# A hybrid SSD / gMLP / MoE layer on one core: the token stage laid out channel-major

## The chip, the core and the metric

One core of a Trainium2 chip runs the whole layer in one launch, all in f32. The metric is device time in microseconds (us), the median of the runs shown; work on the host before and after the launch is not in it.

## The reference, cut to what matters

One layer over 4,096 prompt positions (32 tiles of 128 tokens) and 128 sample positions (8 streams of 16, tile 33). Per tile of tokens x (128 x 1024):

```python
h = rms_norm(x, norm1_g)
proj = h @ w_in                       # 1024 -> 2568 columns
z, xbc, dt_raw, gu, gv = split(proj, [512, 1536, 1544, 2056])
xbc = silu(causal_conv(xbc))          # depthwise, width 4, along tokens, 1024 channels: x 512, B 256, C 256
dt = softplus(dt_raw + dt_bias)       # 8 heads
y = ssd_scan(x, dt, -exp(a_log), B, C) + d_skip * x   # running sums of a*dt, decays, products, a state per head
ssd_out = group_rms(y * silu(z)) * ssm_norm_g
gmlp_out = gelu(gu) * (tril(w_spatial) @ layer_norm(gelu(gv)) + b_spatial)   # chunks of 128 tokens, 8 groups
x = x + concat(ssd_out, gmlp_out) @ w_out
x = x + hier_moe(rms_norm(x, norm2_g))   # top 1 of 4 groups, top 2 of its 8 experts (SwiGLU, 256 wide)
y = rms_norm(x, final_norm_g)
```

It also returns the last three rows that went into the convolution, the SSD states and the sample's v rows.

## The kernel before, in words

The program is written by hand per engine, with semaphores; each engine issues its list in order. It has a token stage (a turn per tile, 33 turns and a closing one) and an expert stage (blocks of 128 routed rows).

**Weights and constants.** `w_in` and `w_out` lie in one `arena` of SBUF, `w_in` as eight row chunks of 2,568 columns; SP loads it in five column groups and VectorE multiplies norm1's gain in (L973 to L977). GpSimd builds identity and masks (L1074 to L1103), small vectors come as rows and are turned by TensorE (L557), the spatial matrices are turned by TensorE and masked by VectorE (L567, L982).

**A turn of TensorE (`pe_turn`, L372)**, for tile i, with the projections of tile i+1 between:

1. eight transposes of `xbc` (token-major, 1,024 channels) to `TB`, which ScalarE copies to `xT`, channel-major, with a halo of three columns (L383, L594);
2. the running sums of a*dt over tokens and their totals (L388, L389), then two 512-column products with a matrix of ones that lay each head's running sum along a row, from `dec` = mask x a*dt that GpSimd wrote (L395, L1061);
3. the first half of the x/B/C projection of the next tile (`project`, L364: eight chunks, 512 columns, hT stationary, weights moving), eight transposes of h2 of the tile before, the second half of x/B/C;
4. B against C (L411), transposes of the activated x and B back to token-major (L416), the router (L490), the spatial mixing (L428), the SSD products (L436, L443, L447);
5. the gv projection, the ranks for routing (L498), the gu projection, eight transposes of x of tile i+2, scaled by its norm before (L457, L850), the z projection;
6. eight transposes of `ycat`, the dt projection of eight columns (L468), and the output projection (L478, two halves), which VectorE adds to `x_res` (L835).

A f32 product of 128 rows stands in the trace as two matmul records, each with a weight load; a transpose as one.

**VectorE (`dve_turn`, L734)** runs the convolution in four passes of eight operations (L758, L760) with h2 after the first, then the decays, the SSD elementwise work, routing (L884), gating, slots (L902), layer norm of v (L852) and the dt chain (L865). **ScalarE (`act_turn`, L577)** copies PSUM banks out and does the activations, among them Gelu of gv and gu (L643, L645), and the copies of the transposed `ycat` to `tT` (L654). **GpSimd (`pool_turn`)** does reciprocal roots, the softplus of dt and the slot scatters. **SP (`sp_turn`, L1117)** queues the loads of x (twice per tile: `x_in` for norm and projection, `x_res` for the residual) and the stores.

**The sample turn** (tile 33) first turns the cached rows, a second set of spatial matrices and 32 state blocks on TensorE (`pe_sample_setup`, L501), with copies by ScalarE.

**The expert stage** gathers 128 rows per block, multiplies with the expert's weights (three loads per expert), adds the residual and scatters each finished block twice, to the prompt's output and to the sample's, rows of the other kind being out of bounds (L1381).

Of the kernel before, what the change touches and what calls it, by code (L numbers as in the profile page):

```python
# [15 lines left out]
F32 = mybir.dt.float32  # L17
I32 = mybir.dt.int32
U32 = mybir.dt.uint32
# [17 lines left out]
CW = 4  # L37
INP = W + CD + H + 2 * W
# [11 lines left out]
N_ROWS = 6  # L50
N_CONST = 3 + 2 + 3 + 2 + 1

W_GROUPS = ((COL_X, 512), (COL_X + 512, 512 + H), (COL_GU, 512), (COL_GV, 512), (COL_Z, 512))
NINIT = NE * T // P // 8
NBLK = 2 * T // P + NE
EPS = 1e-6

# [41 lines left out]
LATER = 8192  # L99
# [6 lines left out]
def build(nc, x_prompt, x_sample, cache_conv, state_ssm, norm1_g, w_in, conv_w, conv_b, dt_bias, a_log,  # L106
          d_skip, ssm_norm_g, ln_v_g, ln_v_b, w_spatial, b_spatial, w_out, norm2_g,
          w_rg, b_rg, w_re, b_re, w_gate, w_up, w_down, final_norm_g,
          y_prompt, y_sample, conv_prompt, ssm_prompt, conv_sample, ssm_sample, gmlp_v_sample):
    ctx = ExitStack()  # L110
    with ctx:
# [6 lines left out]
        def sem(name):  # L118
            return ctx.enter_context(nc.semaphore(name))

# [12 lines left out]
        w_in_sb = arena[:, 0:W_IN].rearrange("p (k n) -> p k n", k=KD)  # L133
# [3 lines left out]
        ident = sb("ident", [P, P])  # L137
        tri = sb("tri", [P, P])
        stri = sb("stri", [P, P])
        tri_s = sb("tri_s", [P, P])  # L140
        blk_s = sb("blk_s", [P, P])
        ones = sb("ones", [P, P])
        row_s = sb("row_s", [P, SB])
        iota_g = sb("iota_g", [P, NG])
        iota_e = sb("iota_e", [P, NE])
        neg_half = sb("neg_half", [P, 2])
        tok_id = sb("tok_id", [P, 1])
        g2_b = sb("g2_b", [P, D])
        lng_b = sb("lng_b", [P, W])
        lnb_b = sb("lnb_b", [P, W])  # L150
        small_b = sb("small_b", [P, 3 * H])
        dtb_b, alog_b, dsk_b = (small_b[:, k * H:(k + 1) * H] for k in range(3))
        aneg_b = sb("aneg_b", [P, H])
        rb_b = sb("rb_b", [P, NR])
        wr_sb = sb("wr_sb", [P, KD, NR])
        wsT = sb("wsT", [P, H, P])
        slot_init = sb("slot_init", [P, NINIT, 2])
# [6 lines left out]
        xbc = sb("xbc", [P, CD])  # L164
        xT = sb("xT", [P, CB, P + CW - 1])
# [3 lines left out]
        gu = [sb("gu", [P, W])] * 2  # L169
        zz = [sb("zz", [P, W])] * 2  # L170
# [11 lines left out]
        rows = h2[0:NROW, 0:P]  # L182
        iota_i = ycat[:, 0:NR + 1].bitcast(I32)
        place_i = ycat[:, 64:64 + NINIT].bitcast(I32)
        slots32 = ycat[:, 0:NE].bitcast(I32)
        dt_t = sb("dt_t", [P, H])
        adt = sb("adt", [P, H])
# [24 lines left out]
        tok0 = sb("tok0", [P, 1])  # L212
        row_i = sb("row_i", [P, 1], I32)
        tok_i = sb("tok_i", [P, P], I32)
        wt = sb("wt", [P, P])
# [8 lines left out]
        dt_p, acs_p, tot_p = MB[:, 0:H], MB[:, H:2 * H], MB[:, 2 * H:3 * H]  # L224
# [3 lines left out]
        smp_bank = [SS[:, 0, :], SS[:, 1, :], YB[:, :]]  # L228

        names = """consts w_scaled eout_a cols_full cols_out ws_full ws_out
            xsq_ready xr_ready x_scaled xT_full xT_out
            proj0 proj1 proj_gv proj_gu proj_z xbc0_out xbc1_out gv_out gu_out z_out
            xbcT_full xbcT_out halo_saved conv_done zs_ready xc_ready cb_done xb_full xb_out
            dt_done dt_read lg_read cb_read rank_read dtneg_ready dtexp_ready dtrec_ready dt_ready trid_ready acs_done bcast_done
# [5 lines left out]
            smp_zero smp_cache_T smp_cache_out smp_ws_T smp_ws_out smp_st_T smp_st_out smp_masks smp_dec_full  # L242
            smp_dec_out smp_new stateT_full stateT_out
# [3 lines left out]
        x_loaded = [sem(f"x_loaded{u}") for u in range(2)]  # L247
        res_loaded = [sem(f"res_loaded{u}") for u in range(2)]
        win_loaded = [sem(f"win_loaded{k}") for k in range(len(W_GROUPS))]
        rows_loaded, const_loaded, wout_loaded = sem("rows_loaded"), sem("const_loaded"), sem("wout_loaded")  # L250
# [3 lines left out]
        smp_loaded = sem("smp_loaded")  # L254
        w_loaded, wd_loaded = sem("w_loaded"), sem("wd_loaded")
# [4 lines left out]
        gf_loaded, slots_set = (sem(n) for n in ("gf_loaded", "slots_set"))  # L260
        dve_step, pool_step = sem("dve_step"), sem("pool_step")

        x_tiles = x_prompt.rearrange("a (t p) d -> (a t) p d", p=P)
        y_tiles = y_prompt.rearrange("a (t p) d -> (a t) p d", p=P)
        x2_tiles = x2_d.rearrange("(t p) d -> t p d", p=P)
        h2_tiles = h2_d.rearrange("(t p) d -> t p d", p=P)
        first_tiles = first_d.rearrange("(t p) d -> t p d", p=P)
# [6 lines left out]
        def input_tile(t):  # L274
            if isinstance(t, int) and t == NP:
                return x_sample.rearrange("b l d -> (b l) d")
            return at_tile(x_tiles, t)


        used = [0]  # L280

        def flat_of(ap):
            return ap.rearrange("p a b -> p (a b)")
# [11 lines left out]
        wsT_s = take(H * P).rearrange("p (h t) -> p h t", h=H)  # L295
        ws_nat = take(H * P).rearrange("p (h t) -> p h t", h=H)
        xT_s = take(CB * SB * (SL + CW - 1)).rearrange("p (b q l) -> p b q l", b=CB, q=SB)
        cache_sb = take(CD)
        adt_e = take(W)
        st_dec = take(4 * SB)  # L300
        sample_end = used[0]
# [1351 lines left out]
```

## Time and profile before

| | us |
|---|---|
| runs | 3192.27, 3192.38, 3183.14 |
| median | 3192.27 |
| profiled execution, its own time | 3190.75 |
| its span in the profile | 3188.9 |

The span goes from the first to the last instruction of the profiled execution; the 1.9 us beside it are launch and end. Times in the trace count from the span's start. A steady turn and the chain through it are read from the view of the chain of waits; the table by stage gives busy time of each engine in a stretch and, as PEclk, the granted clock of TensorE as a share of 2.4 GHz.

### The profile page before, as it was taken

The page shows a single profiled execution, that of the slowest core. Times are in us where ns is not written, and L with a number is a line of the kernel's source. Part 1 is how long each engine was busy: PE and PEld are TensorE (multiplying, and loading weights), DVE is VectorE, ACT ScalarE, POOL GpSimd, SP SyncE. Part 2 cuts the span into 40 slices and gives each one's busy share as a digit, 9 for nine tenths or more (in the row PEclk, how much of TensorE's full clock was granted, in tenths as well). Part 3 has the DMA queues.
Part 4 walks back from the last instruction along what each step waited for, and adds up shares of the span by engine and source line. Part 5 has one row for each costly group of instructions (what it writes and reads, how often), then busy time and mean ns, then how long its engine had stood idle before and what let it go on. Part 6 is the DMA issues. An engine that isn't in the chain of part 4 may idle for free.

```text
span 3188.9 us, 37210 instructions
## 1 busy us (share of the span) xinstructions
PE 3107.2 (97%) x10721; PEld 1686.5 (53%) x10721; DVE 1624.8 (51%) x4412; ACT 876.7 (27%) x1599; POOL 1087.5 (34%) x1988
## 2 busy tenths in 40 slices
PE   7999999999999999999999999996899999999997
PEld 3555565555555555555555555554444444444443
DVE  4454555456554555455544654456344444444444
ACT  2222332223232322233222322221122222222222
POOL 1112112221122112211221111110377767777776
PEclk9999999999999999999999999997899999999999
DMA  7011101101011111010110111023877666767754
GB/s 260 34 40 34 60 33 33 40 33 59 33 40 33 60 33 40 33 60 33 36 37 33 59 34 33 27 72 105 282 236 254 206 207 224 237 198 256 267 170 127
DMA packets 190380, 326.15 MB, mean 102 GB/s; under 512 B 52988, under 2 KB 125241, under 8 KB 190220
## 3 DMA queue, kind: packets, MB, share of 16 engines
q1 hardware_dynamic: 118220, 210.81, 19.5%
q0 software_dynamic: 72000, 113.62, 11.0%
q8 instruction: 50, 0.82, 0.1%
q14 instruction: 110, 0.90, 0.1%
HBM read 283.13 MB, written 182.14 MB: 146 GB/s over the span
## 4 chain that ended last, share of the span: by engine, by line
PE 95%; DVE 1%; DMA 1%; issue 1%; SPq 0%; ACT 0%; POOL 0%; POOLq 0%; DVEq 0%; ACTq 0%
PE PB L369 35%; PE PB L1448 18%; PE PB L478 14%; PE SS L1487 9%; PE TB L358 3%; PE TB L1436 2%; PE YB L436 2%; PE MB L490 2%; PE PB L428 2%; PE SS L395 2%; PE MB L369 2%; PE SS L443 1%; PE SS L447 1%; PE TB L416 1%; PE YB L1480 1%
## 5 line engine op out<-in xcount | busy, mean ns | idle before, releaser
L369 PE MATMUL PB<-arena,hT 128*128 128x512 f32 x2640 | 1164.9, 594 | 3.4 <-DVE arena L976 3.4
L369 PEld LDWEIGHTS PB<-arena,hT 128*128 128x128 f32 x2640 | 495.7, 191 | 578.5 <-issue 574.1
L1448 PE MATMUL PB<-arena,hT 128*128 x1296 | 571.6, 594 | 0.7 <-DMA arena<-in_w_down 0.7
L1001 POOL TENSOR_TENSOR spare<-neg_half 128x1 f32<-128x1 f32 x520 | 102.2, 197 | 1068.4 <-ACT hT L668 615.5
L478 PE MATMUL PB<-arena,tT 128*128 128x512 f32 x1056 | 461.5, 595 | 0.7 <-ACT tT L654 0.7
L1448 PEld LDWEIGHTS PB<-arena,hT 128*128 128x128 f32 x1296 | 247.0, 191 | 312.0 <-issue 312.0
L478 PEld LDWEIGHTS PB<-arena,tT 128*128 128x128 f32 x1056 | 198.1, 190 | 237.7 <-issue 236.8
L1487 PE MATMUL SS<-arena,xdt 128*128 x640 | 287.9, 592 | 0.0
L835 DVE TENSOR_TENSOR x_res<-x_res,PB 128x512 f32<-128x512 f32 x66 | 45.3, 687 | 397.0 <-PE PB L478 397.0
L760 DVE SCALAR_TENSOR_TENSOR xc<-xT,cols,xc 128x128 f32<-128x128 f32 x768 | 210.0, 346 | 2.3
L1362 POOL DMA_INDIRECT out<-arena,lng_b x160 | 171.7, 1073 | 49.2 <-issue 44.9
L1487 PEld LDWEIGHTS SS<-arena,xdt 128*128 128x128 f32 x640 | 115.4, 190 | 114.8 <-issue 114.8
L1516 ACT ACTIVATE xdt<-YB 128x256 f32<-128x256 f32 x80 | 30.7, 384 | 512.1 <-PE YB L1480 512.1
L594 ACT ACTIVATE xT<-TB 128x512 f32<-128x512 f32 x64 | 34.9, 595 | 429.5 <-PE TB L358 429.5
L1545 DVE TENSOR_TENSOR gv<-ycat,PB 128x256 f32<-128x256 f32 x81 | 34.1, 421 | 223.5 <-ACT ycat L1511 222.9
L1048 POOL TENSOR_TENSOR dtw<-dtw 128x8 f32<-128x8 f32 x33 | 6.7, 202 | 346.6 <-DVE dtw L874 346.6
L1005 POOL TENSOR_SCALAR rs<-sq 128x1 f32<-128x1 f32 (+1 forms) x99 | 19.4, 195 | 308.6 <-ACT hT L668 126.3
L1553 DVE SCALAR_TENSOR_TENSOR arena<-arena,rs 128x1024 f32<-128x1024 f32 x80 | 102.4, 1279 | 26.0 <-POOL rs L1389 25.4
L868 DVE TENSOR_TENSOR dtw<-MB,small_b 128x8 f32<-128x8 f32 x33 | 5.5, 167 | 205.1 <-PE MB L369 205.1
L758 DVE TENSOR_SCALAR xc<-xT,cols 128x128 f32<-128x128 f32 x256 | 69.4, 344 | 45.5 <-issue 28.9
L1071 POOL DMA_INDIRECT slot_tokens<-slots x66 | 71.4, 1082 | 48.9 <-DVE tok_id L930 34.5
L775 DVE TENSOR_SCALAR dec<-SS,e_in 128x128 f32<-128x128 f32 x264 | 86.9, 400 | 0.0
(320 smaller groups left out, 4220.2 us busy)
## 6 DMA issues: line engine op xcount, KB each, us to landing
arena<-in_w_gate SPq DMA_DIRECT2D x32, 1024.0 KB
arena<-in_w_up SPq DMA_DIRECT2D x32, 1024.0 KB
arena<-in_w_down SPq DMA_DIRECT2D x32, 1024.0 KB
h_rows<-h SPq DMA_DIRECT2D x34, 512.0 KB, 3.6
x_rows<-x_res SPq DMA_DIRECT2D x33, 512.0 KB, 2.6
first_rows<-g_b SPq DMA_DIRECT2D x33, 512.0 KB, 4.6
x_in<-in_x_prompt SPq DMA_DIRECT2D x32, 512.0 KB, 4.0
x_res<-in_x_prompt SPq DMA_DIRECT2D x32, 512.0 KB, 4.4
```

What stands on the lines that cost most here:

```text
L358: mm = nc.tensor.transpose(TB[b][:, k, :], src(4 * b + k), ident[:])
L369: mm = nc.tensor.matmul(out, hT[u][:, k, :], w_in_sb[:, k, col:col + n], start=k == 0, stop=k == KD - 1)
L478: mm = nc.tensor.matmul(PB[b][:, :], tT[:, k, :], w_out_sb[:, k, b * 512:(b + 1) * 512], start=k == 0, stop=k == KD - 1)
L758: ins = V.tensor_scalar(dst, src, tap[:, w, c:c + 1], cols[:, R_CBIAS + c:R_CBIAS + c + 1], ALU.mult, ALU.add)
L760: ins = V.scalar_tensor_tensor(out=dst, in0=src, scalar=tap[:, w, c:c + 1], in1=dst, op0=ALU.mult, op1=ALU.add)
L775: ins = V.tensor_scalar(dec[:, h, :], SS[:, h // 4, (h % 4) * P:(h % 4 + 1) * P], a, a, ALU.min, ALU.subtract)
L1001: nc.gpsimd.tensor_tensor(spare[:, k:k + 1], neg_half[:, 0:1], neg_half[:, 0:1], ALU.mult)
L1071: nc.gpsimd.indirect_dma_start(out=slot_d[:, :], out_offset=bass.IndirectOffsetOnAxis(ap=slots[:, k:k + 1], axis=0), in_=slots_f[:, 2 + 2 ...
L1362: nc.gpsimd.indirect_dma_start(out=dram, in_=src, in_offset=None, bounds_check=last, oob_is_err=False, out_offset=bass.IndirectOffsetOnAxi ...
L1448: mm = nc.tensor.matmul(PB[u][:, :], hT[u][:, k, :], arena[:, bass.ds(slot + k * 2 * DE, 2 * DE)], start=k == 0, stop=k == KD - 1)
L1487: mm = nc.tensor.matmul(SS[:, n, :], hTb[:, k, :], arena[:, bass.ds(slot + KD * 2 * DE + k * D + n * 512, 512)], start=k == 0, stop=k == 1)
L1553: V.scalar_tensor_tensor(out=f_buf[u], in0=f_buf[u], scalar=rs[:, u:u + 1], in1=gf_b, op0=ALU.mult, op1=ALU.mult).then_inc(s["fin_out"], 1)
```

## The change

- **Host layout.** All inputs come laid out: `x` as rows and once more turned (`x_cols`, per tile the channels in partitions), weights per group with each partition's data in one run, masks, identity and vectors as finished tables, spatial matrices and sample states already turned, gate, up and down of an expert in one array. Outputs y, states and conv rows come back in the kernel's layout and are rearranged on the host; y is one tensor, so a block is scattered once.
- **Turned x.** SP loads `x_cols` straight to hT, once z of the tile before has been projected. TensorE spreads the token's norm factor along a row by one transpose of a repeated column (`pe_spread`), VectorE multiplies hT by it. The eight transposes of x and ScalarE's two copies go.
- **x/B/C channel-major.** `project_channels` takes the weights as stationary operand, 128 channels at a time, and hT as the moving one, 128 columns. ScalarE copies the result straight to `xT`, of which there are two; the eight transposes of `xbc` go.
- **dt.** The gv projection is split: 256 columns of gv together with the eight of dt, and the other 256. The separate dt projection between the transposes of `ycat` and the output projection goes.
- **Running sums.** The sums go to `e_in` after the convolution's first pass; eight transposes of repeated columns spread them, and the totals are read from the last column. GpSimd's product for `dec`, the two products with ones and the product for totals go (the totals stay in the sample turn).
- **Order.** h2 moves behind the convolution's second pass; the spatial mixing writes to `TB[0]`; the first gv half stands between router and mixing; x of tile i+2 is scaled behind the last part of `ycat`.

The new and changed parts of the turn:

```diff
+        def project_channels(pe, u, b, name, done, waits):
+            for sm, v in waits:
+                pe.wait_ge(s[sm], v)
+            for c in range(4):
+                for k in range(KD):
+                    mm = nc.tensor.matmul(PB[b][:, c * P:(c + 1) * P], w_group(name)[:, k, c * P:(c + 1) * P], hT[u][:, k, :],
+                                          start=k == 0, stop=k == KD - 1)
+            mm.then_inc(s[done], 1)
+
+        def pe_spread(pe, t, waits):
+            pe.wait_ge(s["xr_ready"], t + 1)
+            for sm, v in waits:
+                pe.wait_ge(s[sm], v)
+            nc.tensor.transpose(TB[1][:, 0, :], rs[:, 0:1].broadcast_to([P, P]), ident).then_inc(s["rbc_full"], 1)
...
-            transpose8(pe, block_of(xbc), lambda b: [(f"xbc{b}_out", i + 1)] + before(b), "xbcT_full")
-            nc.tensor.matmul(acs_p, cum[:], adt[:], start=True, stop=True)
-            nc.tensor.matmul(tot_p, tot[:], adt[:], start=True, stop=True).then_inc(s["acs_done"], 1)
-            for b in range(2):
-                mm = nc.tensor.matmul(SS[:, b, :], tot[:], flat(dec[:, half(b), :]), start=True, stop=True)
-            mm.then_inc(s["bcast_done"], 1)
+            mm = nc.tensor.matmul(acs_p, tri_s if tn.sample else tri, adt[:], start=True, stop=True)
...
+                project_channels(pe, v, 0, "xa", "proj_xa",
+                                 [("x_scaled", i + 2), ("gu_out", 1) if tn.first else ("x2_half", 2 * i - 1)])
+            pe.wait_ge(s["acs_out"], i + 1)
+            for h in range(H):
+                mm = nc.tensor.transpose(bcast_p[:, h, :], e_in[:, h:h + 1].broadcast_to([P, P]), ident)
+            mm.then_inc(s["bcast_done"], 1)
...
+                project_channels(pe, v, 1, "xb", "proj_xb", [("z_out", 1) if tn.first else ("x2_half", 2 * i)])
...
+            if tn.next:
+                project(pe, v, PB[0][:, 0:NVA], "va", "proj_va", [("xa_out", i + 2)])
...
             if tn.next:
-                project(pe, v, PB[1][:, :], COL_GV, 512, "proj_gv", [("xbc1_out", i + 2)])
+                project(pe, v, PB[1][:, 0:256], "vb", "proj_vb", [("xb_evicted", i + 2)])
...
-                project(pe, v, PB[0][:, :], COL_GU, 512, "proj_gu", [("ycat_hi", i + 1)])
+                project(pe, v, PB[0][:, :], "u", "proj_u", [("va_out", i + 2)])
             if tn.next2:
-                pe.wait_ge(s["x_scaled"], i + 3)
-                transpose8(pe, block_of(x_in[u]), lambda b: [("xb_out", 2 * i + 1 + b)], "xT_full")
+                pe_spread(pe, i + 2, [("xb_out", 2 * i + 2)])
...
-            if tn.next:
-                project(pe, v, dt_p, COL_DT, H, "dt_done", [("cb_read", 1) if tn.first else ("rank_read", i)])
             pe.wait_ge(s["ycT_out"], 2 * (i + 1))
...
+        def act_va(act, t):
+            act.wait_ge(s["proj_va"], t + 1)
+            nc.scalar.activation(gv[:, 0:256], PB[0][:, 0:256], ACT.Gelu_apprx_tanh)
+            nc.scalar.activation(dt_raw[:, :], PB[0][:, 256:NVA], ACT.Copy).then_inc(s["va_out"], 1)
...
+            if tn.next:
+                act.wait_ge(s["mixed_done"], i + 1)
+                act.wait_ge(s["dt_read"], i + 1)
+                act_va(act, i + 1)
+                act_vb(act, i + 1)
...
+                if w == CW - 1:
+                    dve.wait_ge(s["acs_done"], i + 1)
+                    V.tensor_copy(e_in[:, 0:2 * H] if tn.sample else e_in[:, 0:H],
+                                  MB[:, H:3 * H] if tn.sample else acs_p).then_inc(s["acs_out"], 1)
+                if w == CW - 2 and tn.prev:
                     dve_h2(dve, i - 1, v)
...
-            V.tensor_scalar(x_in[u][:, :], x_in[u][:, :], rs[:, 0:1], None, ALU.mult).then_inc(s["x_scaled"], 1)
+        def dve_scale_x(dve, t, j, u):
+            dve.wait_ge(s["rbc_full"], t + 1)
+            dve.wait_ge(xt_loaded[u], 16 * (j + 1))
+            V.tensor_tensor(hT[u][:, :, :], hT[u][:, :, :], TB[1][:, 0:1, :].broadcast_to([P, KD, P]), ALU.mult).then_inc(s["x_scaled"], 1)
...
-            g.tensor_tensor(dec[:, :, :], over(mask, H), adt[:, :].rearrange("p (h a) -> p h a", a=1).broadcast_to([P, H, P]),
-                            ALU.mult).then_inc(s["trid_ready"], 1)
...
+            if tn.next2:
+                sp.wait_ge(s["proj_z"], i + 1)
+                sp.dma_start(flat(hT[u][:, :, :]), at_tile(x_cols, i + 2)).then_inc(xt_loaded[u], 16)
             if tn.next3:
-                sp.wait_ge(s["xT_full"], 2 * (i + 2))
-                sp.dma_start(x_in[v][:, :], input_tile(i + 3)).then_inc(x_loaded[v], 16)
+                sp.wait_ge(s["xsq_ready"], i + 2)
+                sp.dma_start(x_in[v][:, :], at_tile(x_rows, i + 3)).then_inc(x_loaded[v], 16)
...
+                sp.dma_start(xT_s[:, :, :, 0:HALO], cache_in.rearrange("p (b q w) -> p b q w", b=CB, q=SB)).then_inc(cache_loaded, 16)
...
+                sp.dma_start(conv_sample.rearrange("p (b q w) -> p b q w", b=CB, q=SB), xT_s[:, :, :, SL:]).then_inc(convs_stored, 16)
```

## Rows read from the trace of the kernel before

**Rows 1.** The page, part 1: busy us, share of the span, instructions.
```profile
PE 3107.2 (97%) x10721; PEld 1686.5 (53%) x10721; DVE 1624.8 (51%) x4412; ACT 876.7 (27%) x1599; POOL 1087.5 (34%) x1988
```

**Rows 2.** Busy time by stage: stretch, its length, PE, PEld, DVE, ACT, POOL, PEclk, DMA share.
```profile
62.38:128.00 65.62, 64.74 (x211) 35.37 (x212) 28.63 (x74) 16.93 (x28) 7.33 (x20) 0.95 0.03 8
128.00:192.40 64.40, 64.40 (x241) 36.10 (x240) 34.73 (x114) 19.25 (x33) 10.11 (x24) 1.00 0.12 42
2135.10:2204.75 69.65, 56.02 (x227) 39.05 (x227) 41.20 (x121) 17.80 (x44) 5.93 (x7) 0.80 0.08 28
2249.83:3165.00 915.17, 915.17 (x2716) 449.47 (x2717) 425.53 (x488) 226.04 (x474) 640.15 (x625) 1.00 0.68 225
```

**Rows 3.** The chain of waits in one steady turn: start us, us, what.
```profile
971.30 0.87 PE TB L358 x8
...
972.30 0.22 PE MB L389 x2
972.52 1.82 PE SS L395 x4
974.34 6.87 PE PB L369 x16
...
988.95 0.45 PE MB L411 x4
...
991.95 1.81 PE PB L428 x16
...
995.54 0.92 PE SS L443 x4
...
1011.51 0.88 PE TB L358 x8
...
1020.12 1.69 PE MB L369 x16
...
1035.64 0.87 PE TB L358 x8
```

**Rows 4.** The timeline of ScalarE in the turn after it: start us, us, what.
```profile
1063.19 0.19 ACT L668 ACTIVATION_READ_ACCUMULATOR hT<-x_in 128x1 f32 x1
...
1070.60 1.28 ACT L643 ACT_TABLE_LOAD   x1
...
1084.12 1.08 ACT L654 ACTIVATE tT<-TB 128x512 f32<-128x512 f32 x2
```

**Rows 5.** The timeline of VectorE at the turn of two tiles.
```profile
1035.68 0.69 DVE L835 TENSOR_TENSOR x_res<-x_res,PB 128x512 f32<-128x512 f32 x1 [6.11 <-PE PB L478]
1037.24 2.17 DVE L758 TENSOR_SCALAR xc<-xT,cols 128x128 f32<-128x128 f32 x8 [0.87 <-ACT xT L594]
```

**Rows 6.** The chain, the output projections before and after the long turn.
```profile
760.99 13.84 PE PB L478 x32
...
828.63 13.85 PE PB L478 x32
```

**Rows 7.** Busy time in one stretch of that turn, columns as in rows 2.
```profile
797.00:801.00 4.00, 4.00 (x20) 4.00 (x20) 3.44 (x18) 0.00 (x0) 0.00 (x0) 0.50 0.00 0
```

**Rows 8.** The timeline of TensorE at the start.
```profile
16.90 9.66 PE L369 MATMUL PB<-arena,hT 128*128 128x512 f32 x16 [1.83 <-DVE arena L976]
28.15 20.87 PE L369 MATMUL PB<-arena,hT 128*128 128x512 f32 x48 [1.59 <-DVE arena L976]
...
62.38 1.42 PE L358 MATMUL TB<-ident,xbc 128*128 128x128 f32 x8 [3.84 <-DVE wsT L984]
```

**Rows 9.** The timeline of VectorE at the start, scaling the last weights.
```profile
40.88 3.26 DVE L976 TENSOR_SCALAR arena<-arena,cols 128x512 f32<-128x512 f32 x8 [2.12 <-DMA arena<-in_w_in]
```

**Rows 10.** The chain at the start of the sample turn.
```profile
2135.24 0.60 PE SS L506 x8
...
2144.86 2.17 DVE xc L758 x8
```

**Rows 11.** The timeline of GpSimd in the tail.
```profile
3183.61 0.98 POOL L1362 DMA_INDIRECT out<-arena,lng_b  x1 [0.31 <-issue]
```

More of the change, by code:

```diff
@@ L163, in build @@
         hT = [sb(f"hT{u}", [P, KD, P]) for u in range(2)]
-        xbc = sb("xbc", [P, CD])
-        xT = sb("xT", [P, CB, P + CW - 1])
+        xT_mem = [sb(f"xT{u}", [P, CB * SB * (SL + HALO)]) for u in range(2)]
+        xT = [m[:, 0:CB * (P + HALO)].rearrange("p (b t) -> p b t", b=CB) for m in xT_mem]
+        xT_s = xT_mem[0][:, :].rearrange("p (b q l) -> p b q l", b=CB, q=SB)
         xc = sb("xc", [P, CB, P])
@@ L362, in block_of, with project @@
             return lambda c: t[:, c * P:(c + 1) * P]
-        def project(pe, u, out, col, n, done, waits):
+        def project(pe, u, out, name, done, waits):
             for sm, v in waits:
@@ L732, in heads, with over @@
             return ap.rearrange("p (h d) -> p h d", h=H)
+        def over(mask, n):
+            return mask.rearrange("p (a t) -> p a t", a=1).broadcast_to([P, n, P])
         def dve_turn(dve, st, tn):
@@ L983, in dve_phase1 @@
-            for b in range(2):
-                V.tensor_tensor(wsT[:, half(b), :], SS[:, b, :].rearrange("p (h t) -> p h t", h=4), over(tri, 4),
-                                ALU.mult).then_inc(s["ws_out"], 1)
+            dve.wait_ge(ws_loaded, 16)
+            V.tensor_tensor(wsT[:, :, :], wsT[:, :, :], over(tri, H), ALU.mult).then_inc(s["ws_ready"], 1)
             dve.wait_ge(wout_loaded, 16)
@@ L1650, with whole, layer, by_chunk @@
-    build(nc, *args)
-    r = _run(nc, [arrays], core_ids=[0])
-    return tuple(r.results[0][f"out_{i}"] for i in range(len(_OUTS)))
+    def whole(name):
+        return np.asarray(inputs[name])
+    def layer(name):
+        return whole(name)[0]
+    def by_chunk(w):
+        return w.reshape(-1, P, w.shape[-1]).transpose(1, 0, 2)
+    def spread(rows):
+        return np.broadcast_to(rows.reshape(1, -1), (P, rows.size))
+    x = np.concatenate([whole("x_prompt").reshape(SEQ, D), whole("x_sample").reshape(P, D)]).reshape(NT, P, D)
@@ new lines @@
+    w_in = by_chunk(layer("w_in"))
+    b_spatial, ws = layer("b_spatial"), layer("w_spatial")
+    ws_smp = np.zeros((H, P, P), np.float32)
+    for q in range(SB):
+        ws_smp[:, q * SL:(q + 1) * SL, q * SL:(q + 1) * SL] = ws[:, 0:SL, 0:SL]
+    state = layer("state_ssm")
+    lane = np.arange(P)
+    consts = np.zeros((P, NCONST), np.float32)
+    stream = lane // SL
+    same = stream[:, None] == stream[None, :]
+    upper = lane[:, None] <= lane[None, :]
+    for c, mask in ((C_IDENT, lane[:, None] == lane[None, :]), (C_TRI, upper), (C_STRI, lane[:, None] < lane[None, :]),
+                    (C_TRI_S, upper & same), (C_BLK_S, same), (C_ONES, same | ~same)):
+        consts[:, c:c + P] = mask
```

715 lines of the change are left out of this document (310 added, 405 removed).

## The prediction

> **What bounds the kernel now.** I read the page first. TensorE is busy for 97% of the span [rows 1], so the next question is whether it is held up anywhere or simply has that much to issue. The table by stage answers it [rows 2]: in a token turn TensorE is busy for all 64.40 us, while VectorE needs 34.73, ScalarE 19.25 and GpSimd 10.11 and the DMA engines work 12% of the time; in the expert stage it is busy for all 915.17 us. The places where it is not are the sample turn (56.02 of 69.65), the start and the tail. The chain of waits then gives a price for each piece [rows 3]: in a steady turn the chain never leaves TensorE, each piece starts where the one before ended, and from one first piece to the next are 1035.64 - 971.30 = 64.34 us. So a turn costs the sum of what TensorE issues, in its written order, and an edit is worth what it takes out of that sum, as long as no other engine becomes late.
>
> **A turn, term by term** (prices from [rows 3]). Taken out: the eight transposes of xbc (0.87) and of x_in (0.88), the dt projection of eight columns (1.69, as dear as a wide one per weight load), the second running-sum product (0.22) and the two ones-products that spread the sums (1.82). Together 5.48. Put in: eight transposes for the spread, 0.87 by the xbc row, and one of 1/8 of that, 0.11, for the scale row. The gv projection becomes halves of 264 and 256 columns: a pass of 512 takes 6.87/16 = 0.429, half of it 0.215; the 256-column row gives 0.92/4 = 0.23. I take 0.215 and 0.222, since sixteen in a row run like the long one: 7.0 instead of 6.87, +0.12.
>
> The x/B/C projections are the term that the trace does not show at length. Each goes from 16 passes of 512 columns (6.87) to 64 passes of 128, each with a weight load of its own. Bounds: from below 6.87, the same columns with the loads wholly hidden; from above, first the nearest row, the 128-column products of one turn, four passes in 0.45, 0.1125 each, 64 x 0.1125 = 7.20. The transposes run 128 columns at 0.87/8 = 0.109. I take 0.11, so 7.04 each, +0.34 for both. That loads hide behind streaming is seen in the same row: passes of 8 columns cost 1.69/16 = 0.106 and of 64 columns 1.81/16 = 0.113, about what a load alone needs, and 128 columns cost no more, though they stream for a quarter of 0.429 = 0.107 by themselves.
>
> The Trainium skill ("TensorE: Matmul & The Clock Gate", Part 3, The mechanism) says otherwise: weight loads overlap running matmuls only when they address another row group, which full-array matmuls never do. By that rule the change would lose its gain several times over; it is the first rival below. The trace does not agree: 0.1125 for load and streaming together [rows 3].
>
> One wait is new. Today the dt projection stands between the transposes of ycat and the output projection, and covers ScalarE's copies of them to tT. Those copies, 1.08 us from 1084.12, end at 1085.20 [rows 4]; the transposes end at the start of the dt piece, one turn after 1020.12 [rows 3], at 1084.47. With dt gone TensorE stands idle for some 0.8 us there (nothing, if the copies came earlier; 0.8 follows from the rows, so I take it). The sum is -5.48 + 0.98 + 0.12 + 0.34 + 0.80 = -3.24, a turn of 61.1 us.
>
> **Is another engine late in the new order?** Counting TensorE's pieces from the start of a turn: sums 0.1, x 7.2, spread 8.0, h2 8.9, B/C 15.9, the small products and router to 18.9, v-with-dt 22.5, mixing 24.3, the SSD products 27.9, second v half 31.3, ranks, u from 31.7 to 38.6, z to 45.6. VectorE starts the convolution straight after the last residual add (0.73 later, [rows 5]) instead of waiting for transposes and copies (1.6), four passes of 2.17 [rows 5]; h2 now stands after the second pass and is ready at about 6.7 (0.73, two passes, the sums and h2's own 1.3), needed at 8.0. The sums leave PSUM after the first pass, at 3.2, needed at 7.2. The convolution ends at 11 and the activated xc at 12, needed at 15.9. The tightest is u, which overwrites the bank of the first v half: ScalarE must have mixing behind it (24.3) and the square of x_in, which today ends at 1063.38 [rows 4], 27.7 into the turn, and not later in the new one; then it loads its table (1.28, [rows 4]) and evicts v and dt (some 0.8): 29.8, needed at 31.7. GpSimd loses its large product for dec; its dt chain keeps its place beside the output projection. The new wait on SP, for z before the load of the turned x, holds back only loads that are wanted a turn later; the extra 512 KB per turn meet DMA engines at 12% [rows 2]. Scaling hT (two 512-column VectorE operations' worth, about 1.3) waits for the spread at 38.7 and is done by 40, before the last transposes need its bank at 46. So these edits cost nothing beyond the sum; what covers them is TensorE's own queue, and the first to break would be u, with 1.9 us to spare.
>
> **The clock.** Four of the turns are about 3.3 us longer: from 760.99 to 828.63 are 67.64 [rows 6], with a granted clock of 0.50 (the 1.2 GHz level) [rows 7] just after router and mixing, the two pieces with the fewest columns, stood next to each other. All four make 12.6 (2007.1 from 128.0 [rows 2] to 2135.1 less 31 x 64.34). In the new order the v half with its 264 columns stands between them, so I count all 12.6 as gone; the bound is that they stay.
>
> **Outside the loop.** Start: TensorE begins its first projection at 16.90 and the first turn at 62.38 [rows 8]. What goes: dt (1.69), the eight spatial transposes (0.87), idle times of 1.59 and 3.84, and some 2.1 because the first weights come as whole rows without small loads before them; what comes is 0.4. That is 9.7. The last weights landed at 40.88 [rows 9]; their bytes are nearly the same, so the z weights are there by then and the turn can start at 52.7. First turn: 65.62 [rows 2], of which router, ranks and h2 are missing, so it should take 61.4; the extra 4.2 is waiting and cold clock. I take 3.2 + 4.2 = 7.4. Sample turn: the convolution starts 9.6 after the turn does [rows 10], as sixteen transposes of cache and masks and 32 of states come first; those arrive laid out, so 0.8 after. The mask product moves to a later place: -8. Expert stage: TensorE is solid [rows 2], fewer DMAs change nothing there. Tail: one scatter per block instead of two, two fewer at the end, some 1.2 us each with the gap before it [rows 11]: -2.4. The conv cache and conv_sample now move in runs of 12 bytes, 8,192 each; no row prices runs so short. Nothing waits for them before the expert stage, some 90 us on, so I take nothing and leave 10 us of the upper side to them.
>
> **Sum.** The profiled execution took 3190.75, 1.5 below the median of 3192.27. 31 x 3.24 = 100.4; clock 12.6; start 9.7; first turn 7.4; sample 8; tail 2.4: 140.5. 3190.75 - 140.5 = **3050 us**, 4.4% faster.
>
> **Rivals.** *Loads not hidden (slower).* If a 128-column pass pays its load (0.106) and then its streaming (0.107), 64 take 13.6: 6.6 more than I take, twice in 33 turns, +436: 3486. It decides from the point where a projection loses 140/66 = 2.1, a pass of 0.143. Against it stand 0.1125 and 0.109; for it, that no row has more than eight such passes in a run. 6%. *A wait in each turn.* ScalarE's longer queue before u, or the idle time before the output projection, 1 to 2 us worse than I have it: 33 to 66 more, 3083 to 3116. For it: two more cross-engine handovers per turn than before, and PSUM banks that go round faster. 16%. *A dip of the clock in every turn*, behind the sixteen transposes that now stand together (spread, h2) or the new idle time: 33 x 3.3 = 109, 3159; for it, that the new idle time comes behind eight more transposes; against it, that no row dips there and the stretch that did is broken up. 6%. *The change doesn't do what it says:* the dt and transposes leave, but stalls and dips of over 2 us fill their place, and the start gains nothing: a turn of 64.3 and about 3180. 2%.
>
> **How the numbers follow.** Forecast 70%. Its bounds: both projections at 6.87 gives -11, at 7.20 gives +11; start and first turn +-9; dips staying +13; idle time half as much -13. So 3025 to 3080, and the range runs on over the second rival to 3112. About 0.3%, 10 us, is what a measurement can tell from no change: faster 0.92 (forecast, second and third rival), same 0.02, slower 0.06.
>
> **What would show it.** A turn of 61.1 us in the chain; 64 passes of a channel projection in 7.0; one idle of TensorE per turn, 0.8, ended by ScalarE's copy to tT; no stretch at clock 0.50 in mid-loop; first turn from about 53. Wrong if the channel projections take 9 or more, if TensorE waits before u or the spread, or if the clock falls in each turn.

## The result and the profile after

The changed kernel takes **3080.55 us** (median of four runs, 3079.57 to 3082.87) beside 3190.02 for the kernel before (four runs): a ratio of 0.9661, 95% interval 0.9644 to 0.9679. The profiled execution took 3080.07 us, its span 3077.8. Forecast were 3050 with a range of 3025 to 3112: the sign and the range held, the point was 30 us too low. The forecast's own bounds end at 3080; the range reaches further because it was run on over the rival of a wait in each turn.

Part 1 of the page (as [rows 1]: busy us, share, instructions) shows the same picture as before, TensorE busy nearly throughout, with more and shorter passes:

```profile
PE 2964.3 (96%) x13401; PEld 1924.4 (63%) x13401; DVE 1635.4 (53%) x4436; ACT 812.1 (26%) x1517; POOL 911.2 (30%) x1853
```

The table by stage (columns as in [rows 2]), for the start up to the first output projection, the turn after it, the sample turn and the expert stage with the tail:

```profile
0.00:97.22 97.22, 81.22 (x456) 63.24 (x456) 53.13 (x137) 24.71 (x42) 9.41 (x29) 1.00 0.59 237
97.22:158.83 61.61, 60.82 (x322) 43.87 (x322) 35.17 (x115) 17.44 (x32) 8.10 (x23) 1.00 0.14 52
...
2023.80:2081.24 57.44, 44.92 (x169) 32.59 (x169) 35.23 (x112) 12.38 (x22) 8.31 (x20) 0.76 1.08 118
...
2143.08:3077.80 934.72, 918.66 (x2736) 451.39 (x2736) 428.66 (x490) 230.41 (x482) 549.34 (x562) 0.99 0.64 220
```

A turn that was 64.34 is 61.61, and TensorE is busy for 60.82 of it: the idle time of 0.79 is the one that was forecast. Five stretches account for the whole difference of the spans, 111.1 us. Their marks are the first output projection, the last one of the prompt, that of the sample and the first block of the experts; in the kernel before they stand in the chain of waits as

```profile
114.23 13.84 PE PB L478 x32
...
2121.41 13.84 PE PB L478 x32
...
2188.34 7.13 PE PB L478 x16
```

and 2249.83 [rows 2]:

| stretch | before | after | difference | forecast |
|---|---|---|---|---|
| start to first output projection | 114.23 | 97.22 | -17.0 | -17.1 |
| 31 turns | 2007.18 | 1926.58 | -80.6 | -113.0 |
| sample turn | 66.93 | 57.44 | -9.5 | -8 |
| to the first expert block | 61.49 | 61.84 | +0.3 | 0 |
| expert stage and tail | 939.07 | 934.72 | -4.4 | -2.4 |

So one line missed, the turns, by 32.4 us. The chain of waits through two of them, one of each kind (as [rows 3]), shows why:

```profile
968.34 14.00 PE PB L482 x32
...
982.46 7.25 PE PB L375 x64
989.71 0.87 PE SS L405 x8
990.58 0.87 PE TB L355 x8
991.46 7.15 PE PB L375 x64
...
1029.95 14.01 PE PB L482 x32
1044.14 2.79 issue
...
1051.78 0.32 DVE h L808
...
1061.29 0.59 ACT tT L650
1061.93 0.92 PE TB L420 x6
...
1092.91 14.00 PE PB L482 x32
```

From 968.34 to 1029.95 are 61.61, and the chain never leaves TensorE until the copies to tT. From 1029.95 to 1092.91 are 62.96, and here the chain goes through VectorE: 2.79 us of "issue" (time in which the engine waits for nothing that the profile shows), the convolution, h2 (L808), the decays, and by way of ScalarE's copy of the transposed h2 back to TensorE. Twelve of the 31 turns, every second one inside the loop, are of this kind (62.89 to 63.13), and none in the part behind the loop. They make 16.7 us. The remaining 15.7 are 31 times the 0.51 by which a turn without that is longer than the 61.1 of the forecast, less 0.1 for the last turn, which took 61.50.

The timeline of VectorE at the long turn, as [rows 5], and that of TensorE beside it:

```profile
1043.99 0.69 DVE L801 TENSOR_TENSOR x_res<-x_res,PB 128x512 f32<-128x512 f32 x1 [6.11 <-PE PB L482]
1047.14 2.14 DVE L717 TENSOR_SCALAR xc<-xT,cols 128x128 f32<-128x128 f32 x8 [2.47 <-issue]
...
1051.78 1.28 DVE L808 SCALAR_TENSOR_TENSOR h<-x_res,rs,bc 128x1024 f32<-128x1024 f32 x1 [0.20 <-DVE xc L719]
```

```profile
1053.12 1.09 PE L355 MATMUL TB<-cst,h 128*128 128x128 f32 x8 [0.93 <-DVE h L808]
```

Between the last residual add and the convolution VectorE issues nothing for 2.47 us: the body of its loop, two tiles, ends there. TensorE then waits 0.93 for h2. The projection behind it starts 1.14 later in its turn than in a short turn (0.93, and the overlap with the piece before that an idle time ends); the other 0.2 of the long turn's 1.35 come where the transposes of xc wait for ScalarE's copy of the transposed h2 (1061.29 and 1061.93 in the chain above). The same gap stands in the kernel before, in every second turn; its timeline of VectorE a turn ahead of [rows 5]:

```profile
974.40 2.14 DVE L758 TENSOR_SCALAR xc<-xT,cols 128x128 f32<-128x128 f32 x8 [2.38 <-issue]
976.75 1.28 DVE L841 SCALAR_TENSOR_TENSOR h<-x_res,rs,g_b 128x1024 f32<-128x1024 f32 x1 [0.20 <-DVE xc L758]
```

There h2 was ready 976.75 + 1.28 - 971.30 = 6.7 us into the turn and wanted at 974.34 + 6.87 - 971.30 = 9.9, behind the first x/B/C projection [rows 3]: 3.2 to spare.

The view of waits of TensorE (what, on whom: us in total, times, longest) names the two waits that the turns have; twelve of the 14 for h2, 11.6 us, are in the loop:

```profile
PE PB L482 <- ACT tT L630: 26.1, 33, 0.8
PE TB L355 <- DVE h L808: 15.7, 14, 2.6
```

At the start (timeline of TensorE, as [rows 8]) the first turn begins at 52.74, where 52.7 was forecast:

```profile
15.92 16.23 PE L375 MATMUL PB<-hT,arena 128*128 128x128 f32 x128
31.99 20.91 PE L366 MATMUL PB<-arena,hT 128*128 128x264 f32 x64
52.74 0.28 PE L395 MATMUL MB<-adt,cst 128*128 128x8 f32 x2
```

### The profile page after: what moved, and what is told of

The parts are those of the page before. It is cut to its first block, busy times and chain, and to the rows that moved or that the text cites. A ratio compares the mean times of both kernels' runs of the same rounds, so it can differ in the third digit from the quotient of the medians.

```text
span 3077.8 us, 42241 instructions
## 1 busy us (share of the span) xinstructions
PE 2964.3 (96%) x13401; PEld 1924.4 (63%) x13401; DVE 1635.4 (53%) x4436; ACT 812.1 (26%) x1517; POOL 911.2 (30%) x1853
## 4 chain that ended last, share of the span: by engine, by line
PE 88%; DVE 6%; issue 3%; ACT 2%; DMA 1%; POOL 0%; DVEq 0%; SPq 0%; ACTq 0%; POOLq 0%
PE PB L366 22%; PE PB L1359 18%; PE PB L482 15%; PE PB L375 10%; PE SS L1397 9%; DVE xc L719 3%; PE TB L1347 2%; PE YB L444 2%; PE MB L493 2%; PE TB L435 2%; ACT tT L630 1%; DVE dec L741 1%; PE SS L451 1%; PE SS L455 1%; DVE xc L717 1%
## 5 line engine op out<-in xcount | busy, mean ns | idle before, releaser
L366 PE MATMUL PB<-arena,hT 128*128 128x512 f32 (+2 forms) x2112 | 708.9, 490 | 0.0
L366 PEld LDWEIGHTS PB<-arena,hT 128*128 128x128 f32 x2112 | 394.0, 190 | 259.8 <-issue 231.0
L375 PE MATMUL PB<-hT,arena 128*128 128x128 f32 x4224 | 486.7, 276 | 0.0
L375 PEld LDWEIGHTS PB<-hT,arena 128*128 128x128 f32 x4224 | 478.7, 193 | 0.0
L1359 PEld LDWEIGHTS PB<-arena,hT 128*128 128x128 f32 x1296 | 246.2, 190 | 310.6 <-issue 310.6
L965 POOL TENSOR_TENSOR spare<-cst 128x1 f32<-128x1 f32 x520 | 100.3, 193 | 1115.5 <-ACT x_in L645 614.0
L719 DVE SCALAR_TENSOR_TENSOR xc<-xT,cols,xc 128x128 f32<-128x128 f32 x792 | 216.3, 345 | 1.2
L640 ACT ACTIVATE h<-x_res 128x1024 f32<-128x1024 f32 x33 | 34.9, 1057 | 446.6 <-DVE x_res L801 446.6
L814 DVE TENSOR_TENSOR hT<-hT,TB 128x1024 f32<-128x1024 f32 x33 | 40.3, 1221 | 127.6 <-PE TB L384 127.6
L1274 POOL DMA_INDIRECT out_y<-arena,bc x80 | 86.5, 1081 | 24.7 <-issue 23.8
L1437 ACT ACTIVATE h<-arena 128x1024 f32<-128x1024 f32 x80 | 85.4, 1067 | 5.9 <-DVE arena L1459 5.9
```

What stands on the lines that cost most here:

```text
L366: mm = nc.tensor.matmul(out, hT[u][:, k, :], w_group(name)[:, k, :], start=k == 0, stop=k == KD - 1)
L375: mm = nc.tensor.matmul(PB[b][:, c * P:(c + 1) * P], w_group(name)[:, k, c * P:(c + 1) * P], hT[u][:, k, :], start=k == 0, stop=k == KD - 1)
L719: ins = V.scalar_tensor_tensor(out=dst, in0=src, scalar=tap[:, w, c:c + 1], in1=dst, op0=ALU.mult, op1=ALU.add)
L965: nc.gpsimd.tensor_tensor(spare[:, k:k + 1], neg_half[:, 0:1], neg_half[:, 0:1], ALU.mult)
L1274: nc.gpsimd.indirect_dma_start(out=dram, in_=src, in_offset=None, bounds_check=last, oob_is_err=False, out_offset=bass.IndirectOffsetOnAxi ...
L1359: mm = nc.tensor.matmul(PB[u][:, :], hT[u][:, k, :], arena[:, bass.ds(slot + k * 2 * DE, 2 * DE)], start=k == 0, stop=k == KD - 1)
```

## The experiments

Each compares with the kernel before on the same chip; differences given against the changed kernel are between medians. A turn is the distance between the starts of two output projections in the chain.

### VectorE's loop written out

```diff
         def over_tiles(eng, turn, steps=None, per_turn=0):
+            if eng is nc.vector:
+                for i in range(NT + 1):
+                    turn(Turn(i // 2, i % 2))
+                return
```

> VectorE's loop over pairs of tiles is written out, nothing else; the other engines keep theirs. Theory A (the 13 turns of some 63.0 us instead of 61.61 come from the 2.4 to 2.8 us in which VectorE issues nothing at the end of its loop's body, which pushes the convolution and h2 back until TensorE waits): every turn takes 61.6 us, the waits of TensorE for h2 before the transposes (15.7 us in all) go, and the time falls by 16 to 17 us, to about 3064. Theory B (h2's new place behind the second pass is late by itself, or another engine's loop does it): the long turns stay and the time stays within 4 us of 3080.

Measured: 3065.92 us (3062.84 to 3068.63), ratio 0.9607 (0.9593 to 0.9620), 14.6 less than the changed kernel. Theory A: every turn of the loop is 61.61 or 61.62, and the 31 turns are 16.7 us shorter; in the profiled run the start was 0.9 longer. (The long turns are twelve, not thirteen.) The chain through a turn that follows a former loop end:

```profile
1022.34 14.00 PE PB L486 x32
...
1083.96 14.00 PE PB L486 x32
```

The waits for h2 left in the view of waits are those outside the loop:

```profile
PE TB L359 <- DVE h L812: 4.0, 2, 2.6
```

The other four engines kept their loops, TensorE among them. So it is VectorE's loop end alone that cost the time.

The view of DMA queues shows what else happens in the gap. In the changed kernel, from 1044.5 to 1047.3 (queue, kind: packets, MB, share of 16 engines):

```profile
q14 instruction: 1, 0.01, 1.0%
```

One packet of 8 KB of instructions starts 0.4 to 0.7 us after the residual add has ended and takes 0.3 to 0.6 us, in each of the twelve gaps of the changed kernel and of the kernel before. With VectorE's loop written out no packet moves there. The loop is left after its thirteenth pass: no jump back, no gap, and the convolution follows the add at once.

### h2 behind the first pass, where it was

```diff
+                    if tn.prev:
+                        dve_h2(dve, i - 1, v)
...
-                if w == CW - 2 and tn.prev:
-                    dve_h2(dve, i - 1, v)
```

> h2 is put back behind the first pass of the convolution, where it stood before the change; the loop stays. Theory A (loop gap and place of h2 act together): the gap of VectorE stays, the 0.95 us of TensorE's wait for h2 in each long turn go, 13 x 0.95 = 12 us less; some 0.3 us per long turn stay at the transposes of xc, so about 3068. Theory B (the gap is worth its 1.3 us whatever stands behind it, since the whole convolution is late and TensorE only waits elsewhere, for the activated xc): within 4 us of 3080.

Measured: 3091.73 us (3087.62 to 3093.59), ratio 0.9687 (0.9673 to 0.9701): 11 us **slower** than the changed kernel. Neither theory had that time. The waits for h2 are gone from the loop, but the timeline of TensorE in a long turn has another in their place, and the table by stage a stretch right behind it at half the clock:

```profile
314.01 0.92 PE L420 MATMUL TB<-cst,xc 128*128 128x128 f32 x6 [1.17 <-ACT tT L650]
```

```profile
316.00:317.00 1.00, 1.00 (x8) 0.90 (x8) 0.97 (x3) 0.06 (x1) 0.00 (x0) 0.79 0.00 0
317.00:318.00 1.00, 1.00 (x4) 0.79 (x3) 0.93 (x5) 0.00 (x0) 0.00 (x0) 0.50 0.00 0
```

Convolution and decays are as late as in the changed kernel, so ScalarE's copy of the transposed h2, which is queued behind the exponential of the decays, is late too, and the transposes of xc wait for the bank (timeline of ScalarE):

```profile
312.41 1.06 ACT L589 ACTIVATE dec<-dec 128x1024 f32<-128x1024 f32 x1 [0.32 <-DVE dec L741]
313.37 1.07 ACT L650 ACTIVATE tT<-TB 128x512 f32<-128x512 f32 x2
```

The gap's 1.2 to 1.5 us only moved, as theory B had it. But now TensorE stands idle for over a microsecond just ahead of the transposes and the router, and in six of the twelve long turns the granted clock falls to 0.50 (the 1.2 GHz level) under the gv half behind the router: five are 64.5 to 64.8 us, one, in which it falls under the router already, 66.29. The twelve exceed 61.61 by 27.6 us in all, where those of the changed kernel exceed it by 16.7; the 10.9 between are the 11 measured.

### h2 behind the first pass, VectorE's loop written out

The two edits above together.

> h2 behind the first pass, as in the run that became 11 us slower, with VectorE's loop written out. Theory A (the gap alone made the long turns; the place of h2 costs nothing by itself and only decided where TensorE waits, ahead of the transposes of h2 or ahead of the router, where the clock then fell): all turns 61.61, within 4 us of 3066. Theory B (h2 early is worse by itself): above 3072.

Measured: 3065.99 us (3063.88 to 3066.81), ratio 0.9607 (0.9594 to 0.9620): theory A, all turns 61.6. The place of h2 is worth nothing by itself; it decided only where the gap of VectorE came out.

### The same loop written out in the kernel before

> The kernel before, with VectorE's loop over pairs of tiles written out and nothing else. Theory A (the 2.4 us in which VectorE issues nothing at its loop's end cost nothing before, because the convolution was needed later then): turns of 64.34 us as they were, the time within 5 us of 3190, or up to 13 us less if the four turns of 67.65 also came from the gap. Theory B (the gap cost TensorE as much before as after): 15 us less with the turns of 64.34 themselves shorter.

Measured: 3193.22 us (twelve runs, 3187.57 to 3198.96), ratio 1.0016 (1.0005 to 1.0026). Theory A: the interval ends below 1.003, and nothing was gained. VectorE's gap has gone (timeline of VectorE; what it waits for now is ScalarE's copy):

```profile
968.99 2.19 DVE L762 TENSOR_SCALAR xc<-xT,cols 128x128 f32<-128x128 f32 x8 [0.95 <-ACT xT L598]
```

and the turns are 64.34 as they were, with four of 67.65 at other places, so those are not the gap's. The gap was there before and was free; the change made it cost 16.7 us.

### The copies to tT ahead of z, and a wait for each half

```diff
-                act.wait_ge(s["proj_z"], i + 2)
-                nc.scalar.activation(zz[:, :], PB[1][:, :], ACT.Copy).then_inc(s["z_out"], 1)
             for b in range(2):
                 act.wait_ge(s["ycT_full"], 2 * i + 1 + b)
...
+            if tn.next:
+                act.wait_ge(s["proj_z"], i + 2)
+                nc.scalar.activation(zz[:, :], PB[1][:, :], ACT.Copy).then_inc(s["z_out"], 1)
...
-            pe.wait_ge(s["ycT_out"], 2 * (i + 1))
+            pe.wait_ge(s["ycT_out"], 2 * i + 1)
...
+                    if b == 0 and k == 4:
+                        pe.wait_ge(s["ycT_out"], 2 * (i + 1))
```

> ScalarE copies the transposed ycat to tT before it copies z, and TensorE's output projection waits for each half of tT only when it comes to it. Theory A (the 0.8 us of idle TensorE before the output projection is a serial handover of transposes, z copy and two copies, and it also costs the 0.16 us by which that projection is longer, 14.00 instead of 13.84): a turn loses 0.6 to 0.9 us, 20 to 28 us in all, about 3055. Theory B (TensorE then waits for the copies all the same, or the later z copy makes the second half of the projection or the silu of z late): less than 8 us.

Measured: 3064.16 us (3063.91 to 3065.55), ratio 0.9605 (0.9592 to 0.9618), 16.4 less, below the 20 expected. The short turns are 61.07, 0.54 less. The timeline of TensorE shows the idle time down to 0.25 and the projection as long as ever:

```profile
1021.93 14.00 PE L484 MATMUL PB<-arena,tT 128*128 128x512 f32 x32 [0.25 <-ACT tT L630]
```

0.79 - 0.25 = 0.54 is the whole gain, so theory A holds in its first half alone. The first copy runs from 1021.28 to 1021.88, and the last transpose has ended at 1021.68: a handover remains.

### A projection of eight columns back in its place

```diff
+            if tn.next:
+                for k in range(KD):
+                    nc.tensor.matmul(MB[:, 0:H], w_group("va")[:, k, 0:P], w_group("va")[:, k, 256:NVA], start=k == 0, stop=k == KD - 1)
             pe.wait_ge(s["ycT_out"], 2 * (i + 1))
```

> Eight products of 8 columns, as the dt projection had them, are put between the transposes of ycat and the output projection; their result is read by nobody. Theory A (the separate dt projection was worth its 1.69 us less the idle time that it covered): the idle of 0.8 us goes, a turn becomes 1.69 - 0.8 - 0.16 = 0.73 us longer, 33 turns 24 us, about 3105. Theory B (the projection was worth its whole 1.69 us): 56 us, 3136; Theory C (it was hidden): within 5 us of 3080.

Measured: 3105.22 us (3104.71 to 3108.09), ratio 0.9734 (0.9720 to 0.9747): 24.7 more, theory A. Short turns are 62.34, 0.73 more. Chain of waits:

```profile
1040.18 1.69 PE MB L477 x16
1041.87 13.85 PE PB L485 x32
```

The piece takes its 1.69, the idle time is gone, and the output projection is back at 13.85. So of the dt projection's 1.69 us the change kept 0.73 a turn: 0.79 went into the idle time that the piece had covered, the rest into the longer output projection. Most of that rest, 0.14, is overlap: a piece of the chain counts from the end of the piece before, and passes that follow without a wait start 0.14 before that end, which they can't do behind an idle time.

### The first gv half behind the states

```diff
-            if tn.next:
-                project(pe, v, PB[0][:, 0:NVA], "va", "proj_va", [("xa_out", i + 2)])
...
+            if tn.next:
+                project(pe, v, PB[0][:, 0:NVA], "va", "proj_va", [("xa_out", i + 2)])
             if tn.next:
                 project(pe, v, PB[1][:, 0:256], "vb", "proj_vb", [("xb_evicted", i + 2)])
```

> The first gv half (264 columns) moves from between router and mixing to behind the state products, so that router and mixing stand next to each other again, as before the change; nothing else. Theory A (the clock fell in four turns of before because these two pieces with few columns stood together, and the gv half between them cured it): the granted clock falls to 0.50 behind the router again in some turns, each 3.3 us longer, 4 of them 13 us, about 3094. Theory B (the neighbourhood does not matter; the clock falls behind an idle time just ahead of the router, as in the kernel with h2 early, where 1.17 us of idle TensorE and then 0.50 stood there): no more dips than in the changed kernel, within 4 us of 3080.

Measured: 3097.96 us (six runs, 3085.59 to 3120.87), ratio 0.9727 (0.9694 to 0.9760). Two turns of 64.92 in the profiled run, the slower runs with a lower mean clock (0.975 at 3120.87, 0.986 at 3085.59). That is theory A. To see whether the wait in the long turns is needed for it, the same with VectorE's loop written out:

> As the run with the first gv half behind the state products (two turns of 64.92 us with a granted clock of about 0.65 in 380 to 390, times from 3086 to 3121), with VectorE's loop written out too, so that no turn has the wait for h2. Theory A (router, mixing and SSD products next to each other bring the dips, with or without a wait): some turns 3.3 us longer again, and times from 3070 up, spread over 15 us or more. Theory B (it takes the wait of the long turns as well): no dip, all turns 61.61, within 4 us of 3066, as the run with the loop written out alone.

Measured: 3106.10 us (3094.35 to 3106.91), ratio 0.9726 (0.9707 to 0.9745). Theory A again: nine of the turns in the profiled run are 64.91 to 64.93, with no wait for h2 in the loop. The runs spread over 12.6 us, a little under the 15 expected. In the other 22 turns of that execution the clock did not fall, with the same order of pieces; what decides stays open. The table by stage, in mixing and SSD products, first in one of the nine turns, then in the changed kernel:

```profile
1312.00:1316.00 4.00, 4.00 (x18) 3.82 (x18) 3.51 (x18) 0.43 (x2) 0.00 (x0) 0.50 0.00 0
```

```profile
1069.00:1073.00 4.00, 4.00 (x32) 3.85 (x32) 3.43 (x10) 2.76 (x5) 1.07 (x4) 1.00 0.00 0
```

TensorE is busy for all 4 us in both; the clock granted is 0.50 in one and 1.00 in the other, as it was 0.50 in [rows 7].

### The price of a short pass

```diff
+                pe.wait_ge(*((s["z_out"], 1) if tn.first else (s["x2_half"], 2 * i)))
+                for n in range(64):
+                    nc.tensor.matmul(PB[1][:, 0:64], w_group("xb")[:, n % 8, 0:P], hT[v][:, n % 8, 0:64], start=True, stop=True)
                 project_channels(pe, v, 1, "xb", "proj_xb", [("z_out", 1) if tn.first else ("x2_half", 2 * i)])
```

> 64 products more in each of 32 turns, each with a weight load of 128 x 128 and 64 columns, ahead of the second x/B/C projection, which then overwrites their result; it measures the price of a pass by itself. Theory A (a pass costs the longer of its load, 0.106 us, and its streaming, 0.054 for 64 columns): 64 x 0.106 to 0.113 = 6.8 to 7.2 us a turn, 218 to 231 in all, about 3300. Theory B (streaming alone): 3.4 us a turn, 110 in all, about 3190. Theory C (load and streaming one after the other): 10.2 us a turn, 328 in all, about 3405.

Measured: 3537.05 us (3535.73 to 3538.59), ratio 1.1092 (1.1074 to 1.1110). The expectation counted wrongly: 64 f32 products are 128 passes, each with a load, so its sums are for half the work, and doubled the three theories say 13.6 to 14.4, 6.8 to 6.9 and 20.5 us a turn. The chain shows:

```profile
1052.12 14.24 PE PB L413 x128
1066.36 7.20 PE PB L375 x64
```

14.24/128 = 0.111 a pass of 64 columns, beside 7.20/64 = 0.1125 for one of 128: theory A. Turns grew from 61.61 to 75.90. A pass of 8 columns costs 0.106 (1.69/16), one of 64 0.111 and one of 128 0.1125: up to 128 columns a pass costs about what its load does, and the columns stream beside it. The Trainium skill ("TensorE: Matmul & The Clock Gate", Part 3, The mechanism) lets a load overlap, by its list, only where it addresses another row group, and by the paragraph above that list also where it goes to a background weight buffer; full arrays one after the other do not follow the list here.

### A version built on this

VectorE's loop written out, and in TensorE's list:

```diff
-            if tn.next2:
-                pe_spread(pe, i + 2, [("xb_out", 2 * i + 2)])
-            if tn.next:
-                project(pe, v, PB[1][:, :], "z", "proj_z", [("gv_out", i + 2)])
...
+            transpose8(pe, block_of(ycat), lambda b: [("ycat_hi", i + 1)] if b == 0 else [("xb_out", 2 * i + 2)], "ycT_full")
+            if tn.next:
+                project(pe, v, PB[1][:, :], "z", "proj_z", [("gv_out", i + 2)])
+            if tn.next2:
+                pe_spread(pe, i + 2, [("ycT_out", 2 * (i + 1))])
```

with ScalarE's copies to tT ahead of the z copy, and VectorE's scaling of hT behind its dt chain.

> A version built on the findings: VectorE's loop written out, and in TensorE's list the transposes of ycat stand ahead of the z projection and the spread of the norm factor behind it, so that z's 6.9 us cover ScalarE's copies to tT; ScalarE copies tT before z, VectorE scales hT behind its dt chain. Theory A (nothing else is late: ycat is ready 3.5 us before it is then needed): the idle of 0.8 us goes and the output projection takes 13.84 again, a turn of 61.61 - 0.79 - 0.16 = 60.66, 33 x 0.95 = 31 us less than the run with the loop written out alone, about 3035. Theory B (ycat, or the spread that now ends later, becomes late): an idle of over 0.5 us ahead of the transposes or of the next x projection, 3050 or more.

Measured: **3031.81 us** (3029.40 to 3033.87), ratio 0.9508 (0.9493 to 0.9524), 48.7 less than the changed kernel and faster than both kernels. Turns are 60.56. Chain of waits:

```profile
997.78 0.87 PE TB L359 x8
998.65 6.87 PE PB L370 x16
1005.52 0.11 PE TB L388
1005.63 13.73 PE PB L483 x32
1019.36 0.12 PE MB L399 x2
...
1066.18 3.86 PE PB L483 x9
```

Transposes of ycat, z, spread, output projection: no piece waits, and the chain stays on TensorE from turn to turn. The output projection takes 13.73 instead of 14.00. 61.61 - 60.56 = 1.05 is the idle 0.79 and this 0.27.

## Why the prediction was right, and where it was not

- **A turn is what TensorE issues, in order.** Right, and every price removed held: the pieces put in and left (spread and h2 0.87 each, z 6.88) stand in the chain as read from [rows 3].
- **Channel-major projections.** Forecast 7.04 each, measured 7.25 and 7.15: not 0.11 a pass but 0.1125 in the mean, the value of the nearest row, which the text had named as the upper bound (7.20; one of the two lies above it). 0.32 a turn, 10 us. The run of 64 did not come out cheaper than the run of four.
- **The idle time before the output projection.** Forecast 0.80, measured 0.79. What was missing is that the projection behind it takes 14.00 instead of 13.84, 0.16 a turn or 5 us, since an idle time also ends the overlap with the piece before; the run with eight columns back shows both together.
- **The rest of the 0.51.** These two terms are 0.48. The two gv halves were mis-sized too: 3.64 + 3.45 = 7.09 against 6.87, +0.22 where +0.12 was forecast. Mixing came out 0.08 shorter (1.73 for 1.81), which nobody forecast and which hides most of that.
- **Is another engine late?** This is the step that failed: "VectorE starts the convolution straight after the last residual add (0.73 later, [rows 5])", with h2 "ready at about 6.7" and "needed at 8.0", and "the first to break would be u, with 1.9 us to spare". The turn of [rows 5] lies inside the loop's body; at the body's end the delay is 3.1 us, as the row at 974.40 of the kernel before would have said. With it the prediction's own count gives h2 at 6.7 + 2.4 = 9.1 against 8.0 to 8.2: 0.9 late, where 0.93 was measured. h2 broke, in every second turn of the loop, and behind it ScalarE's copy of the transposed h2: by the start of the projection behind h2 the twelve turns are 14.3 us late, by the end of the transposes and the router 16.7. Nothing was seen of u. The runs with the loop written out show it; and the kernel before with its loop written out shows that the gap had been free there, under the 3.2 us of slack that the change took away by wanting h2 earlier and making it later.
- **The rival of a wait in each turn.** Nearest to what came, with 3083 to 3116, but the wait has another cause and stands in 12 turns only. The forecast's own bounds, 3025 to 3080, end just short of the 3080.55; that the stated range held owes more to its extension over this rival than to the account of the turns, and so in part to luck.
- **The clock.** Forecast: all four long turns go, since the gv half stands between router and mixing. Right: none is left, and moving that half away brings them back, with or without waits. Few columns alone are not the reason, though: "the two pieces with the fewest columns" is wrong, as the dt projection has eight to the router's 36 and mixing's 64, and in the run with eight columns back no turn dips. The run with h2 early adds that an idle time ahead of the router can do it too, in six of twelve turns, which the prediction had not.
- **Loads not hidden.** Refuted by 7.15 to 7.25 for 64 passes and by 0.111 for a pass of 64 columns.
- **Start, first turn, sample, tail.** 17.0 for 17.1, 9.5 for 8, 4.4 for 2.4. From TensorE's last product to the end of the span the trace has 16.1 us instead of 18.2, which is the tail's part; where the expert blocks gained the other 2.3 stays open. For the runs of 12 bytes 10 us had been left: no wait for them stands in the view of waits, and the stretch behind the sample turn grew by 0.3.

## What to carry to other kernels

When a change takes work off the path ahead of a consumer, read the producer's start in more than one turn, the turn at a loop's end among them: a gap that costs nothing today is paid when its cover goes. Cover for a handover between engines is best something that has to run anyway: here a projection put between transposes and the product that reads their copies was worth more (1.05 us a turn) than doing the copies sooner (0.54). And look at which pieces with few columns become neighbours, and at the granted clock behind them, before an order is changed.

## What the runs showed of the hardware

- VectorE issued nothing for 2.3 to 2.7 us at the end of its loop's body, in both kernels, once for each of the twelve jumps back and not where the loop is left; TensorE, with a loop of the same kind, lost nothing there (all turns 61.6 with only VectorE's written out). The Trainium skill ("Runtime: NRT & Kernel Launch", Instruction fetch mechanics) says that a taken branch to a place outside the fetched window stalls the engine until it is fetched. The gap at the loop's end agrees with that: a packet of 8 KB of instructions moves in each of the gaps, and none with the loop written out. The packet takes 0.3 to 0.6 us; what fills the rest of the gap no run here shows, and the record of a packet does not name the engine it is for.
- The granted clock fell to 0.50 with TensorE busy throughout, at the end of the mixing and through the SSD products, where router, mixing and these stood together: in 9 of 31 turns of one execution, in 2 of another kernel's, whose runs went from 3086 to 3121 us. With a projection of 264 columns between router and mixing it did not fall there, except, in six of twelve turns, behind an idle time of 1.2 to 1.4 us.
- The same 32 passes of the output projection took 13.73, 13.84 and 14.00 us in the chain, behind a transpose without a wait, behind passes of eight columns, and behind an idle time of 0.25 or 0.79. In the trace the passes start 0.43 apart in all of them; only the step from the first to the second differs, 0.43, 0.51 and 0.53. What is left of the step from 13.84 to 14.00 is the lost overlap of 0.14.
